# Expert rows gathered earlier among other rows, four engine sequences rewritten, and a finer last stretch in a one-core diffusion layer with a product-key expert stage

## What is computed

```python
def peer(h, w_pq, sub_keys, expert_u, expert_v):
    q = (hf @ w_pq).reshape(T, PEER_HEADS, 2, PEER_DK // 2)
    s = jnp.einsum('thpd,hpnd->thpn', q, sub_keys).astype(jnp.float32)
    sv, si = lax.top_k(s, PEER_TOPK)
    ...
    top_s, pos = lax.top_k(cand, PEER_TOPK)
    eidx = jnp.take_along_axis(cidx, pos, axis=-1).reshape(T, PEER_HEADS * PEER_TOPK)
    gates = jax.nn.softmax(top_s, axis=-1).reshape(T, PEER_HEADS * PEER_TOPK)
    act = jnp.einsum('td,nd->tn', hf, expert_u)
    a_sel = jnp.take_along_axis(act, eidx, axis=1).astype(jnp.float32)
    coef = (gates * jax.nn.gelu(a_sel, approximate=False)).astype(h.dtype)
    dense = jnp.zeros((T, N_EXPERTS), h.dtype).at[jnp.arange(T)[:, None], eidx].add(coef)
    return (dense @ expert_v).reshape(B, S, D)
```

## Time and profile before

| what | value |
|---|---|
| device time, median of 3 runs | 1320.39 us (1319.21 to 1320.97) |
| the profiled execution's own time | 1322.54 us |
| its span, first to last instruction | 1320.70 us |
| busy: PE, DVE, POOL, ACT | 1008.7, 875.6, 561.5, 294.3 us |
| moved by DMA | 492.55 MB, mean 373 GB/s |

### The profile page before, as it was taken

One profiled execution on the slowest core, in us unless ns is written; L12 is line 12 of the kernel. 1 busy time (PEld: TensorE's weight loads), 2 busy tenths in 40 slices (PEclk: granted clock), 3 DMA queues, 4 the chain that ended last, 5 costly groups with the idle time before them and its releaser, 6 DMA issues.

```text
span 1320.7 us, 15185 instructions
## 1 busy us (share of the span) xinstructions
PE 1008.7 (76%) x5204; PEld 595.4 (45%) x5204; DVE 875.6 (66%) x2295; ACT 294.3 (22%) x755; POOL 561.5 (43%) x598
## 2 busy tenths in 40 slices
PE   7899989889899987788610386578777877776775
PEld 5757688754567774457300151233323322232322
DVE  0536349999973889523799605996779666666665
ACT  2653335323335443112100011011020000100001
POOL 0010103246676655363767677343333433333331
PEclk9899999999899998889755588789998999999999
DMA  9988368699999999999999999999999999999995
GB/s 384 365 310 320 152 223 333 234 336 413 360 409 384 332 407 358 388 366 361 368 407 409 408 408 411 385 422 422 422 420 419 420 422 422 422 421 422 422 422 208
DMA packets 96539, 492.55 MB, mean 373 GB/s; under 512 B 10704, under 2 KB 11600, under 8 KB 67920
## 3 DMA queue, kind: packets, MB, share of 16 engines
q0 software_dynamic: 83696, 404.26, 76.5%
q1 hardware_dynamic: 12768, 87.33, 16.8%
HBM read 488.93 MB, written 2.62 MB: 372 GB/s over the span
## 4 chain that ended last, share of the span: by engine, by line
PE 44%; DMA 24%; DVE 19%; issue 5%; POOL 4%; ACT 3%; SPq 0%; DVEq 0%; ACTq 0%
PE bank L1293 41%; DMA big<-in_euv,consts 16%; DVE big L2149 7%; DMA wring<-in_euv,consts 5%; POOL big L859 2%; PE bank L1299 2%; DVE extra L2149 1%; PE bank L1322 1%; DVE wring L2149 1%; DVE ops L2149 1%; DVE W L2173 1%; DMA big<-in_ev,rowT 1%; DMA extra<-in_eu,idx 1%; ACT hT L950 1%; DMA big<-in_eu,consts 1%
## 5 line engine op out<-in xcount | busy, mean ns | idle before, releaser
L1293 PE MATMUL bank<-big,W 128*32 128x512 f32 (+1 forms) x932 | 306.5, 677 | 77.9 <-DVE W L2173 56.0
L2149 DVE CUSTOM_DVE_ANT_0 big<-big,hnow 128x1024 f32<-128x1024 f32 x226 | 269.4, 1218 | 71.0 <-DMA big<-in_euv,consts 63.4
L1293 PE MATMUL bank<-wring,W 128*128 128x512 f32 (+1 forms) x456 | 172.7, 626 | 69.5 <-DVE W L2173 68.9
L1293 PEld LDWEIGHTS bank<-big,W 128*32 128x32 f32 (+1 forms) x932 | 106.4, 159 | 242.9 <-issue 238.2
L869 POOL DMA_INDIRECT big<-in_euv,consts x114 | 108.9, 955 | 152.7 <-PE bank L1293 145.1
L2149 DVE CUSTOM_DVE_ANT_0 wring<-wring,hnow 128x1024 f32<-128x1024 f32 x90 | 109.2, 1219 | 69.0 <-DMA wring<-in_euv,consts 67.0
L859 POOL DMA_INDIRECT big<-in_ev,rowT x119 | 113.2, 951 | 76.8 <-issue 36.6
L1293 PEld LDWEIGHTS bank<-wring,W 128*128 128x128 f32 (+1 forms) x456 | 63.3, 170 | 167.4 <-issue 165.9
L869 POOL DMA_INDIRECT wring<-in_euv,consts x76 | 71.8, 944 | 136.6 <-PE bank L1293 130.4
L1293 PE MATMUL bank<-big 128*128 128x128 f32 (+1 forms) x1056 | 117.1, 268 | 12.8 <-DVE big L1910 8.4
L1293 PEld LDWEIGHTS bank<-big 128*128 128x128 f32 (+1 forms) x1056 | 107.6, 181 | 28.8 <-issue 13.3
(11 more groups left out here) (360 smaller groups left out, 1479.8 us busy)
## 6 DMA issues: line engine op xcount, KB each, us to landing
wring<-in_wch SPq DMA_DIRECT2D x23, 2048.0 KB, 11.1
big<-in_wch SPq DMA_DIRECT2D x4, 1536.0 KB, 14.1
dn_tok<-in_wch SPq DMA_DIRECT2D x4, 1536.0 KB, 11.0
tok<-in_wch SPq DMA_DIRECT2D x6, 768.0 KB, 7.6
z<-in_wch SPq DMA_DIRECT2D x6, 512.0 KB, 9.5
gate<-in_wch SPq DMA_DIRECT2D x6, 512.0 KB, 12.2
tok<-in_wch SPq DMA_DIRECT2D x4, 512.0 KB, 15.4
extra<-in_wch SPq DMA_DIRECT2D x4, 512.0 KB, 12.5
```

Of the source, the lines that this page charges most:

```text
L1293: return nc.tensor.matmul(out, lhsT, rhs, start=first, stop=last)
L2149: V.tensor_tensor_reduce(u, u, hnow[:, :], 1.0, 0.0, ALU.mult, ALU.add, coef[t % 2][:, n:n + 1]).then_inc(dot_ready, 1)
```

## The change

Three things are changed.

First, the order of the gathers. 24 U rows of tile 0's second half (ranks 64 to 87) are issued by twos behind each of the V batches 4 to 15 of the first half. The other 40 follow the V batches.

Second, the four sequences of `ORDERS` are written anew. They hold the same steps in another order, apart from those named here. One line of DVE's table and one of POOL's, before and in the change:

```diff
-spread.48 dot.2.34:36 spread.49 dot.2.36:38 spread.50 dot.2.38:40 spread.51 dot.2.40:42 spread.52 dot.2.42:44
+spread.47 dot.2.35:38 spread.50 spread.49 dot.2.38:45 spread.53 spread.51:53 dot.2.45:48 spread.54 dot.2.48:50
...
-gv.0.0.0.0:4 gv.0.0.1.0:4 gv.0.0.2.0:4 gv.0.0.3.0:4 gv.0.0.4.0:4 gv.0.0.5.0:4 gv.0.0.6.0:4 gv.0.0.7.0:4 gv.0.0.8.0:4
+gv.0.0.0.0:4 gv.0.0.1.0:4 gv.0.0.2.0:4 gv.0.0.3.0:4 gv.0.0.4.0:4 gu.0.64:66 gv.0.0.5.0:4 gu.0.66:68 gv.0.0.6.0:4
```

The diff, with the tables left out:

```diff
+FIRST_AMONG, AMONG = 4, 2
...
-LAST = 2
+LAST = 3
+SINGLES = 10
+LAST_LANDS = [ROWS + 8, EXTRA0, EXTRA0 + 1]
...
-TWOS = ([(1, n, n + 1) for n in range(HALF, SLOTS, 2)] + [(2, n, n + 1) for n in range(0, SLOTS - LAST, 2)]
-        + [(2, n) for n in range(SLOTS - LAST, SLOTS)])
+TWOS = ([(1, n, n + 1) for n in range(HALF, SLOTS, 2)] + [(2, n, n + 1) for n in range(0, SLOTS - SINGLES, 2)]
+        + [(2, n) for n in range(SLOTS - SINGLES, SLOTS)])
...
-    out = []
+    out, early = [], 0
     for t, a in HALVES:
-        out += [("gu", t, HALF * a + n) for n in range(HALF)]
-        out += [("gv", t, a, b, j) for b in range(BATCHES) for j in range(QUADS)]
+        out += [("gu", t, HALF * a + n) for n in range(early, HALF)]
+        early = 0
+        for b in range(BATCHES):
+            out += [("gv", t, a, b, j) for j in range(QUADS)]
+            if (t, a) == (0, 0) and b >= FIRST_AMONG:
+                out += [("gu", t, HALF + n) for n in range(early, early + AMONG)]
+                early += AMONG
...
             def half_sums(t):
 
+                nc.scalar.activation(lamv[:, 2:3], rst[:, 0:1], ACT.Sqrt)
                 for h in range(2):
...
+            def v_last(t):
+
+                ends = (SLOTS - 2, SLOTS - 1)
+                for h in range(2):
+                    for n in ends:
+                        if h == 0:
+                            pe.wait_ge(rows_in[row_slot(("gy", t, n))[0]], row_slot(("gy", t, n))[1])
+                            pe.wait_ge(*spread_ready.at(TWO_OF[t, n]))
+                        at = row(row_slot(("gx", t, n))[0])
+                        ins = mm(acc[h][:, :], spread_at(SUMS[t, n]), at[:, D + 512 * h:D + 512 * h + 512], False, n == SLOTS - 1)
+                        if h:
+                            ins.then_inc(vsum_done, 1)
+                    if h == 0:
                         ins.then_inc(*product.next("half"))
```

More of the change, by code:

```diff
@@ L137, in row_homes @@
         if g[0] == "gy":
-            slot = EXTRA0 + g[2] - SLOTS + LAST
+            slot = LAST_LANDS[g[2] - SLOTS + LAST]
             uses[slot] += 1
@@ L213 @@
[L213 to L217, removed]
@@ L246 @@
[L246 to L249, removed]
-gate.0.0.0 dn_s.0.0 z_gate.0 gate.0.0.1 resid.0.0 mod_turn.9 scales.1 resid.0.1 norm.1.0 dn_s.0.1 top_key.0.0
@@ L296 @@
-spread.91 dot.2.120:122 spread.92 dot.2.122:124 spread.93 dot.2.124:126 spread.94 dot.2.126 spread.95 dot.2.127
-spread.96 take.2 last_norm.2
+norm.0.0 mod_turn.2 mod_turn.1 mod_turn.0 mod_turn.3 scales.0 norm.0.1:3 lam channels.0.0 channels.2.0 channels.1.0
+channels.4.0 channels.3.0 channels.6.0 channels.5.0 modulate channels.7.0 channels.9.0 channels.8.0 channels.11.0
+channels.10.0 gate_in decay dn_scale.0.1 dn_scale.0.0 dn_decay.0.1 dn_decay.0.0 dn_scores.0.0 dn_p.0.0.0 dn_scores.0.1
+mod_turn.5 expo.0.0 dn_p.0.1.0 dn_tt.0.0.0 dn_tt.0.1.0 dn_p.0.0.1 diff.0.0 expo.0.1 dn_tt.0.0.1 dn_p.0.1.1 expo.0.2
@@ new lines @@
+diff.0.1 dn_tt.0.1.1 diff.0.2 dn_p.0.0.2 dn_p.0.1.2 dn_tt.0.0.2 dn_tt.0.1.2 dn_p.0.1.3 dn_p.0.0.3 expo.0.3 dn_tt.0.1.3
+dn_tt.0.0.3 dn_p.0.0.4 dn_p.0.1.4 diff.0.3 dn_full.0.0:2 dn_p.0.0.5 dn_p.0.1.5 dn_p.0.0.6 dn_p.0.1.6 head_norm.0.0
+dn_o.0.0:2 head_norm.0.1 gate.0.0.0 dn_s.0.0 z_gate.0 gate.0.0.1 resid.0.0:2 norm.1.0 mod_turn.9 scales.1 dn_s.0.1
+top_key.0.0 pair_sums.0.0.0 top_pair.0.0.0 places.0.0.0 channels.0.1 chosen.0.0.0.0:2 experts.0.0.0 channels.3.1
+channels.2.1 channels.1.1 dot.0.0 top_key.1.0 channels.6.1 dot.0.1 pair_sums.0.0.1 channels.5.1 channels.4.1 dot.0.2
@@ new lines @@
+top_pair.0.0.1 channels.7.1 places.0.0.1 dot.0.3:6 channels.8.1 chosen.0.0.1.0 channels.10.1 chosen.0.0.1.1 dot.0.6
+key_norm channels.9.1 experts.0.0.1 channels.11.1 key_scale.1 top_key.2.0 pair_sums.0.1.0 dn_scale.2.1 key_scale.2
+dot.0.7:10 expert_rows.0.0 dot.0.10 dn_decay.2.1 dot.0.11:14 dn_scores.2.1 dn_p.2.1.0 top_pair.0.1.0 slot_gates.0.0
+dot.0.14:16 rope.1.0 mod_turn.11 dn_p.2.1.1 dot.0.16:19 dn_p.2.1.2 top_key.3.0 dn_p.2.1.3 dot.0.19:22 dn_p.2.1.4
+dn_scale.1.0 dot.0.22:25 dn_p.2.1.5 dot.0.25:36 dn_p.2.1.6 dot.0.36:39 places.0.1.0 dot.0.39:44 dn_decay.1.0
@@ new lines @@
+dot.1.92 spread.12 dot.1.93 spread.14 dot.1.94:96 spread.15 dot.1.96:100 spread.16 dot.1.100:104 spread.17:19
+dot.1.104:109 spread.20 spread.19 dot.1.109:112 spread.23 spread.21 dot.1.112:115 spread.22 spread.24 gate.1.1.1
+last_norm.0 dot.1.115:121 spread.26 spread.25 dot.1.121 spread.27:29 dot.1.122:128 spread.29 spread.31 dot.2.0:2
+spread.30 spread.32 take.1 dot.2.2:4 slot_gates.2.1 dot.2.4:6 spread.33 dot.2.6:8 spread.34 dot.2.8:12 spread.35:37
+dot.2.12:15 spread.37 dot.2.15:19 spread.38 dot.2.19:21 spread.39 spread.41 dot.2.21 spread.40 dot.2.22:25 spread.42
@@ new lines @@
+dot.2.84:89 spread.73 dot.2.89 spread.76 spread.74:76 dot.2.90:92 spread.77 dot.2.92:98 spread.78:80 dot.2.98:102
+spread.80 spread.82 dot.2.102:104 spread.81 dot.2.104:106 spread.83 dot.2.106:111 spread.86 spread.84 dot.2.111
+spread.85 dot.2.112:114 spread.87 dot.2.114:116 spread.88 dot.2.116:118 spread.90 spread.89 dot.2.118 spread.91
+dot.2.119:121 spread.93 spread.92 dot.2.121:123 spread.94:96 dot.2.123 spread.96 dot.2.124:126 spread.97:99
+dot.2.126:128 spread.100 spread.99 take.2 last_norm.2
```

209 lines of the change are left out of this document (98 added, 111 removed).

## The result

The changed kernel takes 1362.97 us (median of 4 runs, 1359.49 to 1368.68) beside 1320.68 us for the kernel before: the ratio is 1.0338, with a 95% interval of 1.0315 to 1.0362. It is slower by 42 us. The forecast was slower by 12 us, 1332 us with a range of 1313 to 1342, so the direction was right and the size was not.

What follows compares the result with a forecast made beforehand. The prediction took the wide rows to be bound by the DMA transfer. Its terms, 19 - 1 - 2.4 - 1.4 - 2.5 = 11.7 us, added to the profiled 1322.54 gave 1334.2, as a median 1332 us, range 1313 to 1342.

Steps and rivals of the forecast that it cites:

- The ten named places: Wide rows of tiles 1 and 2: ten spreads stand behind six later dots, losing 19 us together.
- the price of a place: Wide rows: a spread six ranks late leaves a lead of 3.3 or 2.7 us, losing 1.6 or 2.2 us.
- The rule from row 74: Wide rows: a row issued 4.9 us ahead of its predecessor's landing costs nothing; a shorter lead loses the difference.
- "nothing is lost" at a lag of five: Wide rows: a spread five ranks late leaves a lead of 5.2 to 5.8 us, so nothing is lost.
- the first gathers: Ahead of the first U row: no step leaves the chain, so 0, with 2 us either way.
- The middle: 24 U rows among V batches, up to `resid.2.1`: 1 us of gain, between 5 gained and 3 lost.
- The second rival: Middle gains all its gaps: tile 2's w_out done 9 us sooner, total 1323 us or a little less; chance 0.12.
- the third rival: V batches land late, PE's DeltaNet steps wait, `resid.2.1` slips by up to 8 us: 1340 us; chance 0.10.
- The V rows: V rows behind `resid.2.1`: the 10.26 us wait at 627.03 shrinks, gaining 2.4 us, between 0 and 4.
- The end: Last stretch: first take starts earlier and the table load leaves the chain, gaining 2.5 us, between 1.5 and 3.
- Row 74: Tile 1's wide row 74, late through tile 2's expert choice: that work moves into idle time, 1.4 us come back.
- The first rival: Wide rows: a lead of 3.2 us suffices, so late rows cost only 3 us: 1316 us, down to 1311; chance 0.22.

Runs made afterwards that it cites:

- a lag of six: Kernel before, with the spread of a pair standing behind the dot six ranks later at eight places of tile 2's wide rows: 1341.94 us.
- lags of four: Kernel before, with the spread of a pair put off by four ranks at eight places of tile 2's wide rows: 1318.10 us.
- the run with the clock held up: Changed kernel plus 71 groups of dummy matmuls where PE waits for late spreads: 1351.59 us; where 1.4 us a place is cited, the eight-place run: 1329.95 us.
- with the clock held up at eight places: Kernel before with spreads six ranks late at eight places of tile 2, plus four small dummy matmul groups on PE at each place: 1329.95 us.
- regular spreads: Changed kernel with only DVE's and ACT's wide-row sequences put back, each spread right behind its own pair's second dot, gelus in order: 1329.74 us.
- the last stretch alone: Kernel before with only the change's three narrow last ranks, single gelus and spreads for ranks 118 to 127, and small root ahead of the sums: 1316.13 us.

## Why the prediction was wrong

**Right: the place, the mechanism and the sign.** The spreads that stand behind dots of later ranks make the wide rows late. Putting them back removes all of that loss. The ten named places are where the trace loses most: from landing to landing, over the late row and the two behind it, 2.2 to 4.3 us each and 31 us together (0.5 us at the same rows before). With a lag of six put into the kernel before, a place costs 3.0 us. One sign it named tells little by itself: the median time from issue to landing of a wide row fell to 10.0 us, but with lags of four it is 13.5, and nothing is lost.

**Wrong: the price of a place.** The failed step is the sum "14.92 + 1.30 + 0.61 + 0.15 + 1.84 + 0.28" us, and in it the 1.84 us for PE, half of a pair in the earlier trace rows. That row is of a PE that waited 1.30 us; the late spread makes it wait 7.9 and 9.5 us in the timelines above, and then the slot takes 3.7 us at a granted clock of 0.50. So the leads were shorter than worked out: at the ten places 0.95 to 2.80 us, 1.8 in the mean, where the sum had 2.7 or 3.3; in the run with the clock held up they are 2.9 in the mean. And a place cost some 3 us, not 1.6 to 2.2. The Trainium skill, "TensorE: Matmul & The Clock Gate", section "HAM oscillation — how this bites in real kernels", warns of this: a wait between groups of matmuls lets the clock fall to 1.2 GHz. These traces agree (0.50 behind waits of 7.88 and 9.54 us, above). The prediction did not draw on it, though it spoke against this change. The rule from row 74, that a lead of 4.9 us is needed, held: 4.9 less 1.8 is 3.1, and with the clock held up at eight places a place cost 1.4 us against 1.6. The clock is not all: with it held up in the changed kernel, the wide rows still lose 27.3 us beside regular spreads, where 19 were booked. What the other 8 are made of was not taken apart; the next two points are part of it.

**Wrong: "nothing is lost" at a lag of five.** Instead of 5.2 to 5.8 us the leads at the eight places were 3.6 to 4.7, after a slot at half clock, and they cost 3.9 us together. In the changed kernel 18 pairs have a lag of five; nine of their rows lose nothing, the others 0.2 to 2.7 us. With the 31 us of the ten places that is of the size of the 38.5.

**Wrong: the count.** The table has an eleventh place with a lag of six, rank 14 of tile 2, and it stands two ranks behind that of rank 12, so the places are not all four ranks apart. The trace loses 3.1 us at the two together, so little hangs on it.

**Wrong: the first gathers, "0, with 2 us either way".** It was reasoned from the steps alone. The order of the same steps cost 4 us in the profile and 9 at the median.

**The middle: -1 forecast, +3.8 in the two profiles, +5.5 by the means of all.** The second rival's gain did not come, and for the third rival's late batches nothing speaks: of PE's waits over 2.5 us between the first gather and `resid.2.1` in the changed kernel none is put down to a landing. Some 3 us came of what was named beside this term, DeltaNet's steps behind later dots: it was named for `dn_p.2.0.6` with "5 us, less the gap that is filled", and the first wait was at `dn_o.1.1`, behind rank 90 instead of 86.

**The V rows: -2.4 forecast.** Behind `resid.2.1` the changed kernel's profile is 6.1 us quicker to the first wide row, row 74's 1.4 us not counted. Here too the profile before is the slowest of its kind: 284.2 us, where five runs with the same sequences (those with lags and the last stretch alone) take 280.3 to 282.2, and the five with the change's 277.8 to 281.6. By the means the gain is 1.9 us, so the term came out near its size, but not as reasoned: more was there to gain, and most of it was given back at 740 to 770 us, in a gap that the prediction had not looked for. **The end: -2.5 forecast,** -2.9 in the trace and -2.4 alone on the chip. **Row 74:** its wait of 15 us is gone.

**The first rival** (a late row is hidden) is refuted by the lag of six. The rule that stood beside it, from the Trainium skill, "DMA: Bandwidth & Descriptors", section "Anatomy of one DMA — SWDGE (gpsimd) path", by which a lead of 1.9 us would do by estimate, is off here: with leads near 3.3 us the run with the clock held up still lost 1.4 us a place, and wide row 114, issued at 1307.65, landed 6.1 us later where the rule gives 4.4.

## To carry to other kernels

Where a queue of transfers is the bound, count for each slot how long it is held: a sequence that puts off one small step by a few ranks costs nothing up to a point (here four ranks of ten slots), half a microsecond a time just behind it (five ranks) and 3 us at six. In pricing a late step, price what follows at the clock that its wait leaves behind, not at that of the busy row. And when a wait is removed, look at which next step stands behind the same late work, for a gain here was twice handed back one step or one stage later.

## What was not expected of the hardware

- PE's granted clock fell to 0.50 within a wait of 7.88 us and stayed there for the first slot of the burst; small matmul groups of 1.6 us with pauses of 0.9 us kept it at 1.00.
- Ahead of the first gather the clock fell to 0.50 at about 114 us, at a wait of PE of only 0.75 us (it was busy for 3.25 of the 4 us from 112 on). It came back at about 120 us in one execution; in another, with the same instructions, it came back at about 122, fell again at 125 and stayed at 0.50 until 142.
- A place with a late row often loses time twice, at the late row and at the one behind it: rows 114 and 115 land 5.1 and 3.4 us behind their predecessors, where 2.49 is usual. Row 115 was issued at 1309.77, 3.9 us ahead of row 114's landing, which is under 4.9 too. Why it was late was not tried on its own.
